# Splitting the first modulation in two: half of the features first, the rest inside the first product

## The reference

```
for cond in (c, c_ctx):
    sh_a, sc_a, g_a, sh_f, sc_f, g_f = split(silu(cond) @ mod_w[0] + mod_b[0], 6)   # 6 x 1024
hx = rms_norm(x,   norm_mix_g[0]) * (1 + sc_a) + sh_a
hc = rms_norm(ctx, norm_mix_g[0]) * (1 + csc_a) + csh_a
projections = [hx; hc] @ ev_w_in          # 1024 -> 1984 columns, then attention, w_out, ffn, ...
```

## Time and profile before

| | us |
|---|---|
| median of 3 runs | 2352.18 |
| lowest and highest run | 2349.44, 2352.38 |
| span of the profiled execution, first to last instruction | 2345.6 |
| PE busy in the span | 2246.2 (96%) |
| DVE, ACT busy | 1482.8 (63%), 1019.0 (43%) |

### The profile page before, as it was taken

The page is one execution under the profiler, slowest core; times in us unless marked ns, Lnnn a source line. Parts: engine busy times, 40 slices in busy tenths (PEclk is TensorE's granted clock), DMA queues, the critical chain, the costliest instruction groups (busy, mean ns, idle before and its releaser), DMA issues. The chain is left out here.

```text
span 2345.6 us, 32826 instructions
## 1 busy us (share of the span) xinstructions
PE 2246.2 (96%) x14070; PEld 1930.2 (82%) x14070; DVE 1482.8 (63%) x1880; ACT 1019.0 (43%) x1236; POOL 0.2 (0%) x4
## 2 busy tenths in 40 slices
PE   6998989999998999999999999999999999999997
PEld 3765667777786878999889877999988988789997
DVE  4777543333346567655778767675678777767576
ACT  4255442112225346434574445443556534445354
POOL 0000000000000000000000000000000000000000
PEclk9999989999998999999999999999999999999999
DMA  8540034444423252455655554455555555455552
GB/s 329 198 162 1 19 143 173 176 162 189 162 101 115 90 144 73 163 197 199 222 191 206 189 183 144 180 196 186 196 196 193 194 184 202 147 177 184 189 191 106
DMA packets 61704, 389.97 MB, mean 166 GB/s; under 512 B 6640, under 2 KB 11128, under 8 KB 16376
## 3 DMA queue, kind: packets, MB, share of 16 engines
q1 hardware_dynamic: 61560, 387.88, 45.6%
HBM read 386.79 MB, written 1.06 MB: 165 GB/s over the span
## 5 line engine op out<-in xcount | busy, mean ns | idle before, releaser
L1688 DVE TENSOR_TENSOR w_lo<-raw,w_hi 128x2048 fp32r<-128x2048 f32 x300 | 683.1, 2290 | 483.2 <-ACT w_hi L1222 481.2
L1222 ACT ACTIVATE w_hi<-raw 128x2048 fp32r<-128x2048 f32 x300 | 571.7, 1914 | 686.3 <-PE PS L516 348.0
L514 PE MATMUL PS<-x_hi_lo,w_hi 128*128 128x256 f32 (+1 forms) x2112 | 638.3, 302 | 16.6 <-DVE w_lo L1688 8.1
L515 PE MATMUL PS<-x_hi_lo,w_lo 128*128 128x256 f32 (+1 forms) x2112 | 634.6, 300 | 0.0
L516 PE MATMUL PS<-x_hi_lo,w_hi 128*128 128x256 f32 (+1 forms) x2048 | 609.3, 298 | 0.0
L514 PEld LDWEIGHTS PS<-x_hi_lo,w_hi 128*128 128x128 f32 x2112 | 399.2, 189 | 45.2 <-issue 23.9
L515 PEld LDWEIGHTS PS<-x_hi_lo,w_lo 128*128 128x128 f32 x2112 | 399.9, 189 | 16.4
L516 PEld LDWEIGHTS PS<-x_hi_lo,w_hi 128*128 128x128 f32 x2048 | 386.9, 189 | 14.2
L514 PE MATMUL PS<-w_hi,x_hi_lo 128*128 128x512 f32 (+1 forms) x800 | 319.7, 400 | 22.4 <-DVE w_lo L1688 11.5
L516 PE MATMUL PS<-w_lo,x_hi_lo 128*128 128x512 f32 (+1 forms) x800 | 315.1, 394 | 0.0
L515 PE MATMUL PS<-w_hi,x_hi_lo 128*128 128x512 f32 (+1 forms) x800 | 314.8, 393 | 0.0
(11 more groups left out here) (308 smaller groups left out, 2131.1 us busy)
## 6 DMA issues: line engine op xcount, KB each, us to landing
raw<-chunks_in SPq DMA_DIRECT2D x348, 1024.0 KB, 4.8
bias_ring<-brows_in SPq DMA_DIRECT2D x32, 256.0 KB, 5.0
G<-nrows_in SPq DMA_DIRECT2D x2, 1536.0 KB, 6.7
BIG<-rel_in SPq DMA_DIRECT2D x4, 512.0 KB, 7.6
free_b<-rel_in SPq DMA_DIRECT2D x4, 512.0 KB, 7.9
tabt<-tabs_in SPq DMA_DIRECT2D x1, 1280.0 KB, 10.5
X<-x_in SPq DMA_DIRECT2D x1, 1024.0 KB, 8.7
X<-ctx_in SPq DMA_DIRECT2D x1, 1024.0 KB, 10.8
```

Of the source, the lines that this page charges most:

```text
L514: pe.matmul(o, lhs[0], rhs[0], start=start, stop=False, **more)
L515: pe.matmul(o, lhs[1], rhs[0], start=False, stop=False, **more)
L1222: act.activation(w_hi[:, i % HI_RING, :], ring[:, n % RING, :], ACT.Copy).then_inc(*hi_ready.now(n))
L1688: dve.tensor_tensor(w_lo[:, c % RING, :], ring[:, c % RING, :], w_hi[:, i % HI_RING, :].bitcast(F32), ALU.subtract).then_inc(*lo_ready.now(c))
```

## The change

- Pack 0 is now blocks 0 and 2 (shift and scale of the features 0 to 511), with a turn and a modulation of its own; pack 1 is blocks 1 and 3 (features 512 to 1023). All later packs move up by one number.
- The chunks are stored in the order: modulation chunks 0 to 5 (blocks 0, 2, 1), the first `ev_in` chunk (now 6, was 8), modulation chunks 7 and 8 (block 3), the second `ev_in` chunk (9, was 10), two modulation chunks, and then two behind every `ev_in` chunk (was 1, 2, 2, 2, 1, 2). By the third `ev_in` product both orders have given out 18 modulation chunks.
- PE turns pack 0 right behind the root, before chunks 4 and 5. Chunks 7 and 8 are used inside the first product, behind feature tile 0, and the turn of pack 1 is behind feature tile 1.
- ACT makes the high part of the first chunk in four pieces of 512 columns between the modulated tiles 1 to 4; before tile 4 it copies pack 1 and waits for the second modulation. DVE makes the low part in four pieces, and after the fourth does the second modulation. PE waits for each piece.
- The table loads stay in front of chunk 11; the expression is rewritten to the same number (2 x 4 + 3).

```diff
-MOD_PARTS = (((0, 1, 2, 3), (4, 5, 6, 7, 10, 11), (8, 9)), (tuple(range(12)),))
-MOD_PACKS = [(0, (0, 1, 2, 3)), (0, (4, 5, 6, 7)), (0, (10, 11)), (0, (8, 9)),
+MOD_PARTS = (((0, 2), (1, 3), (4, 5, 6, 7, 10, 11), (8, 9)), (tuple(range(12)),))
+MOD_PACKS = [(0, (0, 2)), (0, (1, 3)), (0, (4, 5, 6, 7)), (0, (10, 11)), (0, (8, 9)),
...
@@ PE
                             for kt in range(KC):
+                                if len(split) == 1:
+                                    pe.wait_ge(*lo_ready.after(c, kt))
                                 pe.wait_ge(*copied_v.after(tiles_of, kt))
...
+                                if at_tile and kt < KC - 1:
+                                    at_tile(kt)
...
+                def upper_mods(kt):
+                    if kt == 0:
+                        mod_chunk()
+                        mod_chunk()
+                    elif kt == 1:
+                        mod_end(0, 1)
...
-                ev_in(0, mods(1, 2), ("mix", 0))
+                ev_in(0, mods(0, 2), ("mix", 0), upper_mods)
                 ev_in(1, mods(2, 2))
...
-                ev_in(2, mods(1, 2))
+                ev_in(2, mods(2, 2))
...
             root_of_squares(("mix", 0), 4, 0)
-            for _ in range(4):
-                mod_chunk()
             mod_end(0, 0)
+            mod_chunk()
+            mod_chunk()
             even_mixer()
...
@@ ACT
+            def split_part(kt):
+                n, cols = chunks[0], slice(kt * NC_, kt * NC_ + NC_)
+                act.activation(w_hi[:, 0, cols], ring[:, n % RING, cols], ACT.Copy).then_inc(*hi_ready.now(n, kt))
...
                 for k in range(KD):
+                    if by_half and k == 4:
+                        high(3)
+                        split_part(3)
+                        modulation(1)
+                        act.wait_ge(*mods_ready.after(l, part + 1))
                     act.wait_ge(*scaled.after(key, k))
...
-                    if k:
+                    if k and not (by_half and k == 4):
                         high(k - 1)
+                    if by_half and 0 < k < 4:
+                        if k == 1:
+                            split_to(0)
+                        split_part(k - 1)
                     if k == 4 and middle:
                         middle()
...
             modulation(0)
-            split_to(first_ev)
-            norm_mod(("mix", 0), 4, 0, lambda: split_to(first_ev + 1))
+            norm_mod(("mix", 0), 4, 0, lambda: split_to(first_ev + 1), True)
...
@@ DVE
-            norm_mod(("mix", 0), 4, KD, (0, 0), None, lambda: lo_to(ev))
+            def at_front(k):
+                if k < KC:
+                    lo_part(k)
+                if k == KC - 1:
+                    modulation(0, 1)
+                    lo_to(ev)
+
+            norm_mod(("mix", 0), 4, KD, (0, 0), at_front)
             lo_to(ev + 1)
...
@@ lay_out
-            mod_next(8)
+            mod_next(6)
...
-                mod_next((1, 2, 2, 2, 1, 2)[n])
+                mod_next(2)
```

More of the change, by code:

```diff
@@ L449, in mod_rows_of @@
         def mod_rows_of(n):
-            at = (0, 512, 1536)[n] if n < 3 else (n % 4) * 512
-            return mod_row_bufs[0 if n < 3 else 1][:, at:at + 512]
+            at = (0, 1024, 512, 1536)[n] if n < 4 else (n % 4) * 512
+            return mod_row_bufs[0 if n < 4 else 1][:, at:at + 512]
         def gain_of(key, k):
@@ L499, in take_chunk @@
                 split.append(c)
-                pe.wait_ge(*lo_ready.after(c))
+                if hi_slot or len(split) > 1:
+                    pe.wait_ge(*lo_ready.after(c))
                 return c, tuple(a.rearrange("p (k n) -> p k n", k=k_tiles) for a in (w_hi[:, hi_slot, :], w_lo[:, c % RING, :]))
@@ L521, in project_tok @@
             def project_tok(st, l, n, k_tiles, lhs, groups=1, freed=stored, n0=0, biased=False, need=None, between=None,
-                            width=NC_, tiles_of=None, side=None, deep=None):
+                            width=NC_, tiles_of=None, side=None, deep=None, at_tile=None):
                 deep = deep or range(-(-k_tiles // KC))
@@ L816, in mod_turn @@
                 for s in range(4):
-                    mm = pe.matmul(by_row[:, js[0]:js[-1] + 1, s, :], rows[:, s * P:s * P + P], sel, start=True, stop=True)
+                    mm = pe.matmul(by_row[:, js[0]:js[-1] + 1:js[1] - js[0], s, :], rows[:, s * P:s * P + P], sel, start=True, stop=True)
                 mm.then_inc(*mod_turned.now(n))
@@ L829, in mod_chunk @@
                 i, last = MOD_PACKS[n][1].index(j), len(MOD_PACKS[n][1]) - 1
-                b = 5 + n % MOD_BANKS
+                b = 5 + (n + 1) % MOD_BANKS
                 first = i == 0 and kg == 0
@@ L874, in even_mixer, with ev_in @@
             def even_mixer():
-                def ev_in(j, mods, tiles_of=None):
+                def ev_in(j, mods, tiles_of=None, at_tile=None):
                     project_tok("ev_in", 0, 1, KD, tokens(hT[4]), 2, n0=j, tiles_of=tiles_of, between=mods,
-                                width=NC_ if j else EV_C)
+                                width=NC_ if j else EV_C, at_tile=at_tile)
+                def upper_mods(kt):
[4 more added lines that the diff above has]
+                        mod_end(0, 1)
                 def mods(first, second):
@@ L902, in turn_dak @@
                     if kg == 0:
-                        mod_end(0, 1)
+                        mod_end(0, 2)
                         pe.wait_ge(*pre_turn.after("dak"))
@@ L959, in _ @@
             root_of_squares(("mix", 0), 4, 0)
-            for _ in range(4):
-                mod_chunk()
             mod_end(0, 0)
+            mod_chunk()
+            mod_chunk()
             even_mixer()
             project_feat("w_out", 0, 2, y4T, width=512, freed=updated("w_out", 0), need=copied("y0"), between=mod_row)
-            mod_end(0, 2)
+            mod_end(0, 3)
             root_of_squares(("ffn", 0), 4)
@@ L1147, in _ @@
                     sp.dma_start(X[:, 1, :, :], ctx_d).then_inc(*x_in.now(by=16))
-                if c == 2 * len(MOD_PARTS[0][0]) + 3:
+                if c == 2 * sum(len(js) for js in MOD_PARTS[0][:2]) + 3:
                     sp.dma_start(tabt[:, EARLY_TABS:], tabs_d[:, EARLY_TABS:]).then_inc(*tab_in.now(by=16))
@@ L1221, in split_to @@
                         act.wait_ge(*projected.after("used", chunks[i - HI_RING]))
-                    act.activation(w_hi[:, i % HI_RING, :], ring[:, n % RING, :], ACT.Copy).then_inc(*hi_ready.now(n))
+                    if i:
+                        act.activation(w_hi[:, i % HI_RING, :], ring[:, n % RING, :], ACT.Copy).then_inc(*hi_ready.now(n))
+            def split_part(kt):
+                n, cols = chunks[0], slice(kt * NC_, kt * NC_ + NC_)
+                act.activation(w_hi[:, 0, cols], ring[:, n % RING, cols], ACT.Copy).then_inc(*hi_ready.now(n, kt))
             def split_up_to(c):
@@ L1285, in root_mod, with norm_mod @@
                                scale=1.0 / D).then_inc(*std_ready.now(key))
-            def norm_mod(key, tiles, part, middle=None):
+            def norm_mod(key, tiles, part, middle=None, by_half=False):
                 l, kind = key[1], 0 if key[0] == "mix" else 3
@@ L1382, in modulation @@
                 act.wait_ge(*projected.after("mod", n))
-                if n >= 4:
+                if n >= 5:
                     act.wait_ge(*mod_turned.after(n - 4))
-                act.activation(mod_rows_of(n), PS[:, 5 + n % MOD_BANKS, :], ACT.Copy).then_inc(*mod_rows.now(n))
+                act.activation(mod_rows_of(n), PS[:, 5 + (n + 1) % MOD_BANKS, :], ACT.Copy).then_inc(*mod_rows.now(n))
             def swiglu(l, tiles):
@@ L1410, in ffn_step @@
                 if n in (4, 8, 12):
-                    modulation(3 + n // 4)
+                    modulation(4 + n // 4)
                 split_to(at + 2)
@@ L1444, in _ @@
             root(("daq", 1), 16, 64)
-            modulation(1)
+            modulation(2)
             split_to(first_ev + 6)
@@ L1468, in _ @@
             split_to(first_ev + 8)
-            modulation(2)
+            modulation(3)
             copy_turned("daq")
@@ L1502, in _ @@
                     split_to(first + 4)
-            modulation(3)
+            modulation(4)
             root_mod(("ffn", 0), 4)
-            norm_mod(("ffn", 0), 4, 2, lambda: split_to(first + 5))
+            norm_mod(("ffn", 0), 4, 3, lambda: split_to(first + 5))
             swiglu(0, 4)
@@ L1686, in lo_to @@
                     c = chunks[i]
+                    if i == 0:
+                        continue
                     dve.wait_ge(*hi_ready.after(c))
@@ L1689, in lo_to, with lo_part @@
                                       ALU.subtract).then_inc(*lo_ready.now(c))
+            def lo_part(kt):
+                c, cols = chunks[0], slice(kt * NC_, kt * NC_ + NC_)
+                dve.wait_ge(*hi_ready.after(c, kt))
```

(17 more changed lines are left out.)

1 line of the change is left out of this document (added).

## The result

| | before | changed |
|---|---|---|
| median, us | 2355.39 (14 runs) | 2363.79 (14 runs) |
| lowest and highest | 2348.54, 2365.04 | 2356.38, 2371.0 |
| ratio | | 1.0041, 95% interval 1.0025 to 1.0056 |
| same kernels in a second set, ratio | (29 runs) | 1.0031, 1.0014 to 1.0048 (12 runs) |
| span of the profiled execution | 2345.6 | 2368.6 |

The kernel became slower by 0.4%: 0.0041 x 2355 = 9.7 us (5.9 to 13.2), in the second set 7.3 us (3.3 to 11.3). The forecast was 2352.18 + 8.7 = 2360.9. The first three runs of the changed kernel have a median of 2366.49, outside the forecast range of 2355 to 2365; with all 14 the median, 2363.79, is inside. The profiled execution took 2370.35 us, 1.75 more than its span, so what lies around the instructions is 1.75 us and not the 6.6 that front and prediction took from a median.

What follows compares the result with a forecast made beforehand. PE (TensorE), busy 96% of the span, was taken as the bound. Terms -2.15 + 1.85 + 1.06 - 0.96 + 6.3 + 1.75, directly 7.7, plus 0.96 gave 8.65 us: 2360.9 us, range 2355 to 2365.

Steps and rivals of the forecast that it cites:

- the hole: Before the first product's second half: PE stands 6.9 us instead of 0.61, from 51.2 to 58.15.
- loads: Tables and chunk 12 issued 20 us later but hidden, 1.6 us to spare; cost 0, up to 2 us.
- The start of the first product: PE's first product at the front starts at 36.5 instead of 38.67, 2.15 us earlier.
- Chunks 7, 8 and the turn on PE's path: Inside the first product nothing hides two modulation chunks, 1.85 us, and the second turn, 1.06 us.
- The cold restart: First product's second half: PE restarts at the low clock for 3.9 us, costing 1.75 us; bounds 0 and 2.4.
- tables in the way: Rival: at 51.2 the load queue is slower, chunk 12 and DVE's store late; 1 to 3 us more, 2363; chance 0.12.
- the one sign of being wrong that showed: Before the second product: PE waiting long for the load of chunk 12 near 72 us would show the forecast wrong.
- Nothing here could absorb it: Behind the first product: later work follows PE's products, so the lag of 8.65 us stays to the end.
- Partly given back: Rival: clock holds across the stand before the second half (-1.75), wait before 143.01 warm (-2.4); 4.5 us slower, 2356.7; chance 0.12.
- The span goes from 2345.6 to 2354.3: Whole profiled execution: the front's 8.65 us added to the earlier span; with 6.6 us around it, 2360.9 us.
- No hole: Rival: second modulation reaches ACT's tile 4 by about 40.5, second half undelayed; +0.15 us, 2352.3; chance 0.14.
- sum +0.15: Ideal case with PE alone as limit: -2.15 + 1.85 + 1.06 - 0.61 = +0.15 us, so no gain.

Runs made afterwards that it cites:

- both turns ahead: Changed kernel with all eight modulation chunks and both turns back ahead of the first product, loads ordered as before; ratio to before 0.9989, median 2351.07 us.
- Next split ahead: Changed kernel with high and low part of the second weight chunk made ahead of the second modulation; ratio to before 1.0057, median 2365.13 us.
- tables early: Changed kernel with the table loads in front of chunk 9 instead of chunk 11; 2358.4 us in one run.

## Why the prediction failed, and what of it was right

The mechanism was right: the hole, its size and its cause came out as forecast. What failed is the last step of the sum, which laid a lag on a level from three runs and on one profiled execution, and put at nothing what executions of one kernel differ by; and before it the term "loads", put at 0, and the sentence that nothing further on could absorb the lag.

- **The start of the first product.** Forecast 36.5 (2.15 us earlier); measured 35.76, with 0.61 added 36.37. The price of a piece was 0.52, as taken from the row. The rule of the Trainium skill's page "ScalarE: Activation LUTs" (section "Rules for kernel authors"), from which the prediction worked out 0.72, is for an activation whose bias is a pointer operand; the pieces are plain copies, so it was not the price to hold against them. The trace has 0.61 for one of them and 0.52 from start to start.
- **Chunks 7, 8 and the turn on PE's path.** Forecast 1.85 and 1.06; measured to the start of what follows 1.85 (40.18 to 42.03) and 0.80 (44.58 to 45.38). Right, and "both turns ahead" shows that their place is the cost. The other turn, of pack 0, was taken as 1.06 in the shadow and took 1.71 (25.92), which no one waits for here but "both turns ahead" does.
- **The hole.** Forecast: fifth pair 47.15, second half 58.15, hole 6.9; measured with 0.61 added 46.97 and 57.96, hole 6.84. "Next split ahead" shortened the chain and the hole with it. Right.
- **The cold restart.** Forecast 1.75 us, measured 1.47, in the second profile 70.11 - 58.37 - 9.91 = 1.83. The size is no constant: behind the same hole it was 12.67 - 9.91 = 2.76 in "tables early", above the bound of 2.4, so a forecast this near was partly luck.
- **Loads: cost 0, 1.6 us to spare. Wrong.** Measured 1.22 and 0.72 us. I let PE need only the low part of chunk 12, and left out that on DVE the store that frees the banks stands behind it: 1.04 us for its first copy. And chunk 12 landed some 1.2 us later than my 65.8 (66.42 + 0.61): from 53 to 65 us the loads ran at 410 GB/s, not at the 434 that I took. The rival "tables in the way" was half of the case, and its sign, a wait behind chunk 12 near 72, is the one sign of being wrong that showed, in a small size.
- **"Nothing here could absorb it". Wrong by 0.6 us.** The old wait of 0.62 at 77.65 is gone in the changed kernel, because its load is issued when PE has used chunk 11, ahead of the new wait of 1.22, and so had that much more time. In "tables early", where the new wait is gone, one of 0.95 stands there. So 7.2 at the seam (68.73 + 0.61 - 62.13) + 1.22 - 0.62 + 0.96 = 8.8; the table has 8.9. The forecast of 8.65 came out near by luck: two errors that cancel.
- **"Partly given back": not across the hole, once near 143.** PE was cold behind the hole in both profiles. In the first profile of changed the lag falls from 9.3 at 140 us to 8.3 at 150, as PE is back at full clock at 155.8, where the 148.5 of before and the lag would give 157.8; in the second it stays at 9.2 to 9.3. What was given back there, once, was 1 us, not the rival's 2.4.
- **The span goes from 2345.6 to 2354.3. Wrong.** It was 2368.6. This is the step of the sum that failed: a lag of one front, laid on one profiled execution, doesn't give the next profiled execution. The difference of executions was a term put at nothing, and it measured 14 us here, beside the 9 of the change. 2.2 us came from one more cold stretch near 231 us, 6.9 and 6.0 us from the slow spacing in two stretches. The second profile of changed has 2355.5, beside the forecast.
- **The level.** I called 2352.18 the time of before and 6.6 us what lies around the span. Three runs gave no hint of the scatter: 14 runs have a median of 2355.39, and the surrounding is 1.75. The profiled execution of before, 2345.6 + 1.75, was shorter than any of the 14. This is the whole miss of the median: 2355.39 + 8.65 = 2364.0, beside the measured 2363.79. The range, too, held only the rivals' terms and nothing for the scatter, and 14 runs of the changed kernel lie between 2356.38 and 2371.0.
- **No hole, sum +0.15.** "Both turns ahead" is that case: 1.1 us behind in the front and no change in total. That splitting the modulation has nothing to win holds for the orders tried; the shadow turned out fuller than I had it.

## What to carry to other kernels

Before moving work out of a shadow (time in which an engine waits anyway) to start a product earlier, follow the whole product: if its second half waits for a serial chain on another engine, the end of that chain decides, and a link of it that now waits for work queued inside the product moves everything behind it. A load that stands in order behind a ring's wait inherits every change of what the ring waits for; look for the second limit before shortening the first, or its gain is taken at the next wait. Where runs scatter by more than the effect, pair the matmuls of two traces and read the lag by stage; a single pair of spans told 23 us here, where 9 belonged to the change.

## What was not expected of the hardware

At full granted clock, back-to-back 256-column matmuls ran at 113.3 or at 117.8 ns, 4% apart, the slow one held for stretches of some 150 to 190 us, in both kernels and changing from execution to execution (885 against 851 matmuls in the same 100 us). Of ten profiles, four had at least one slow stretch. And the phase of the clock at the front differed between two profiles of one kernel by some 2 us (chunks 7 and 8 took 1.92 and 2.52 us), which moved everything behind by 1 us. The Trainium skill's page "TensorE: Matmul & The Clock Gate", section "What's actually happening", says that the moment at which the clock rises is not tied to the kernel's start and differs from run to run; the two profiles agree. The 0.5 us that it names for the difference is less than the 2 us here.
